# Two attention heads per output step, a ring of four score buffers, and other queues for the last stores

## What is computed

```python
z = jnp.einsum('bqhd,bkhd->bhqk', qblk, k) * scale + bias
mask = key_idx[None, :] < qpos[:, None]
log_1mb = jnp.where(mask, jax.nn.log_sigmoid(-z), 0.0)
acc = lax.cumsum(log_1mb, axis=3, reverse=True) - log_1mb
wts = jnp.where(mask, jnp.exp(jax.nn.log_sigmoid(z) + acc), 0.0)
return jnp.einsum('bhqk,bkhd->bqhd', wts, v)
```

## Time and profile before

| | us |
|---|---|
| median of 3 runs | 2250.02 |
| lowest and highest | 2247.71, 2251.95 |
| the profiled execution, its own time | 2249.7 |
| its span, first to last instruction | 2248.1 |
| mean granted TensorE clock | 0.986 of full |
| PE busy | 2185.9 (97%) |
| DVE busy | 1068.2 (48%) |
| ACT busy | 770.7 (34%) |
| POOL busy | 67.7 (3%) |
| `stick()` on PE, from `score(0)` to the end of `sample_outputs` | about 1698.6 to 1792.3 |

### The profile page before, as it was taken

One profiled execution on the slowest core, in us unless ns is written; L12 is line 12 of the kernel. 1 busy time (PEld: TensorE's weight loads), 2 busy tenths in 40 slices (PEclk: granted clock), 3 DMA queues, 4 the chain that ended last, 5 costly groups with the idle time before them and its releaser, 6 DMA issues.

```text
span 2248.1 us, 44698 instructions
## 1 busy us (share of the span) xinstructions
PE 2185.9 (97%) x18380; PEld 2124.4 (94%) x18380; DVE 1068.2 (48%) x1534; ACT 770.7 (34%) x1062; POOL 67.7 (3%) x143
## 2 busy tenths in 40 slices
PE   8999999999988999999999999999999899999996
PEld 7999999998877899999999999999996599999996
DVE  5444433586455554444334444433568444444332
ACT  5222222335244442222223222222357543222222
POOL 0000000100100000000000000000103200000000
PEclk9999999999988999999999999999999999999998
DMA  4333333432300332333233233323324323333331
GB/s 133 97 89 88 91 94 79 123 85 76 81 2 2 90 93 86 93 93 91 88 93 94 86 91 93 89 88 95 99 76 142 114 76 104 93 93 88 90 94 47
DMA packets 353651, 197.89 MB, mean 88 GB/s; under 512 B 10054, under 2 KB 348130, under 8 KB 353544
## 3 DMA queue, kind: packets, MB, share of 16 engines
q1 hardware_dynamic: 344640, 172.36, 26.6%
q0 software_dynamic: 6736, 21.97, 3.2%
q10 hardware_dynamic: 2176, 2.15, 0.3%
HBM read 188.52 MB, written 8.05 MB: 87 GB/s over the span
## 4 chain that ended last, share of the span: by engine, by line
PE 91%; DVE 4%; ACT 2%; issue 2%; DMA 1%; POOL 0%; DVEq 0%; ACTq 0%; POOLq 0%
PE PS L2174 81%; PE PS L2282 5%; PE PS L2849 1%; DVE wlo L1382 1%; PE PS L2768 0%; PE PS L2782 0%; DVE rawE L1419 0%; PE PS L2751 0%; PE PS L2834 0%; DVE tmp L1504 0%; PE PS L2654 0%; DMA tmp<-q_rows 0%; PE PS L2350 0%; PE PS L2189 0%; DMA prow_f<-in_ln_ffn 0%
## 5 line engine op out<-in xcount | busy, mean ns | idle before, releaser
L2174 PE MATMUL PS<-hh,whi 128*128 128x260 f32 x3600 | 730.9, 284 | 2.9 <-DVE hl L2099 1.7
L2174 PE MATMUL PS<-hh,wlo 128*128 128x260 f32 x3600 | 727.2, 284 | 0.0
L2174 PE MATMUL PS<-hl,whi 128*128 128x260 f32 x3600 | 726.3, 283 | 0.0
L1382 DVE TENSOR_TENSOR wlo<-stage,whi 128x1024 fp32r<-128x1024 f32 x337 | 412.3, 1223 | 449.5 <-ACT whi L778 439.7
L2174 PEld LDWEIGHTS PS<-hh,whi 128*128 128x128 f32 x3600 | 557.4, 189 | 5.8 <-DVE small L1521 1.5
L2174 PEld LDWEIGHTS PS<-hh,wlo 128*128 128x128 f32 x3600 | 556.6, 189 | 0.0
L2174 PEld LDWEIGHTS PS<-hl,whi 128*128 128x128 f32 x3600 | 555.2, 189 | 0.0
L778 ACT ACTIVATE whi<-stage 128x1024 fp32r<-128x1024 f32 x337 | 352.7, 1048 | 269.9 <-PE PS L2174 263.0
L2174 PE MATMUL PS<-act_h,whi 128*128 128x260 f32 x1408 | 284.3, 283 | 0.0
L2174 PE MATMUL PS<-act_h,wlo 128*128 128x260 f32 x1408 | 283.5, 283 | 0.0
L2174 PE MATMUL PS<-act_l,whi 128*128 128x260 f32 x1408 | 282.8, 282 | 0.0
(11 more groups left out here) (431 smaller groups left out, 1573.1 us busy)
## 6 DMA issues: line engine op xcount, KB each, us to landing
stage<-in_ffn_w_gate SPq DMA_DIRECT2D x88, 512.0 KB, 3.8
stage<-in_ffn_w_up SPq DMA_DIRECT2D x88, 512.0 KB, 3.8
stage<-in_ffn_w_down SPq DMA_DIRECT2D x64, 512.0 KB, 4.0
stage<-in_w_in_e SPq DMA_DIRECT2D x28, 512.0 KB, 3.8
stage<-in_ffn_w_down SPq DMA_DIRECT2D x32, 384.0 KB, 3.4
stage<-in_w_in_o SPq DMA_DIRECT2D x20, 512.0 KB, 3.7
stage<-in_w_out_e SPq DMA_DIRECT2D x8, 512.0 KB, 3.6
stage<-in_w_out_o SPq DMA_DIRECT2D x8, 512.0 KB, 3.6
```

The lines of the kernel that those rows point to most:

```text
L1382: dve.tensor_tensor(wlo[:, slot, :], stage[:, s % STAGE_SLOTS, :], whi[:, slot, :].bitcast(F32), ALU.subtract).then_inc(lo_ready, 1)
L2174: mm = pe.matmul(psum[:, half, :], w, x(k)[:, half * HALF:(half + 1) * HALF], start=first and w is hi and x is rhs_hi, stop=last and w is lo)
```

## The change

Three edits.

1. Outputs of heads 2m and 2m+1 are made together, `output(m)`, on PE after `sums(h)` of the next even head h = 2m+2 (the last pair within `sample_outputs`). For each of the four widths, the product of the even head (lower 64 partitions of bank 6) stands next to that of the odd head (upper 64). ACT then copies 128 partitions once per pair. As a head's weights now live longer, `skZ` becomes a ring of four, and `skL` moves to another place in memory to make room. `sample_outputs` is cut 4 and 4 around the last pair, where it was 2 and 6 around the last head.
2. POOL stores the prompt's values and keys in turn 6 of its loop, not in turn 4, that is behind the load of the last query row.
3. `y_prompt` is stored by SP in four quarters, not by POOL in two halves, and `y_sample` by SP after them. The copies to `ysrow` are made by DVE, not ACT.

```diff
-                    if n == TS // 2:
+                    if n == TS - 2:
                         pool.wait_ge(v_rows, 1 + NB)
                         save(o["sbv_p"][0, 0].rearrange("(c p) h d -> p c (h d)", p=P), vtok[:])
...
-                    if h >= 3:
-                        act.wait_ge(sk_o, h - 2)
-                    act.activation(skZ[:, h % 3, :], banks(0, 3)[:, 0:SCORES], ACT.Identity, bias=sbb[:, 0, h:h + 1])\
+                    if h >= 4:
+                        act.wait_ge(sk_o, h - 3)
+                    act.activation(skZ[:, h % 4, :], banks(0, 3)[:, 0:SCORES], ACT.Identity, bias=sbb[:, 0, h:h + 1])\
...
+                def output(m):
+
+                    act.wait_ge(sk_o, 2 * m + 2)
+                    act.activation(prO[:, OQ + m, 0:TP], banks(6, 1), ACT.Copy).then_inc(sk_oc, 1)
+                    act.wait_ge(sk_oc, m + 1)
+                    act.activation(oO[:, OK + m, 0:TP], prO[:, OQ + m, 0:TP], ACT.Copy).then_inc(o_hi, 1)
...
-                    if h >= 1:
-                        output(h - 1)
+                    if h >= 2 and h % 2 == 0:
+                        output(h // 2 - 1)
...
-                def output(h):
+                def output(m):
 
-                    r = slice(h % 2 * HDC, (h % 2 + 1) * HDC)
-                    if h:
-                        pe.wait_ge(sk_oc, h)
-                    pe.wait_ge(sk_w, h + 1)
+                    if m:
+                        pe.wait_ge(sk_oc, m)
+                    pe.wait_ge(sk_w, 2 * m + 2)
                     for c, (at, w) in enumerate(SCORE):
-                        mm = pe.matmul(banks(6, 1)[r, c * P:TP], vtok[:, c, h * HDC:(h + 1) * HDC],
-                                       skZ[:, h % 3, at:at + w], start=c == 0, stop=c == NB - 1)
-                    mm.then_inc(sk_o, 1)
+                        for q in range(2):
+                            h, r = 2 * m + q, slice(q * HDC, (q + 1) * HDC)
+                            mm = pe.matmul(banks(6, 1)[r, c * P:TP], vtok[:, c, h * HDC:(h + 1) * HDC],
+                                           skZ[:, h % 4, at:at + w], start=c == 0, stop=c == NB - 1)
+                            if c == NB - 1:
+                                mm.then_inc(sk_o, 1)
...
-                sample_outputs(0, 2)
-                output(HC - 1)
-                sample_outputs(2, TS)
+                sample_outputs(0, 4)
+                output(KC - 1)
+                sample_outputs(4, TS)
...
+            for a in range(4):
+                sp.wait_ge(y_row, KD // 4 * (a + 1))
+                part = slice(a * DM // 4, (a + 1) * DM // 4)
+                sp.dma_start(o["y_prompt"][0].rearrange("(b p) n -> p b n", p=P)[:, :, part], yrow[:, :, part])\
+                  .then_inc(stored, 16)
+            sp.wait_ge(ys_row, 2)
+            sp.dma_start(o["y_sample"][:, 0, :], ysrow[:]).then_inc(stored, 16)
+            sp.wait_ge(stored, 80)
```

More of the change, by code:

```diff
@@ L332, in build_step @@
         of_sample = sb("of_sample", [P, PAGES, TS], F32, st)
+        skL = sb("skL", [P, SCORES], F32, st)
         st.close()
@@ L336, in build_step @@
         VALUE_BANKS, KEY_BANKS = (3, 4, 5, 7), (6, 3, 4, 5)
-        skL = sb("skL", [P, SCORES], F32, st)
         skX = sb("skX", [P, 2, SCORES], F32, st)
-        skZ = sb("skZ", [P, 3, SCORES], F32, st)
+        skZ = sb("skZ", [P, 4, SCORES], F32, st)
         skR = sb("skR", [P, 3 * P], F32, st)
@@ L411, in build_step @@
             sem(n) for n in "gate_read gate_ready up_read prod_ready act_hi act_lo".split())
-        y_row, stored = sem("y_row"), sem("stored")
+        y_row, ys_row, stored = sem("y_row"), sem("ys_row"), sem("stored")
         y_t, SETUP_T = setup_t, 4 + KD
@@ L753, in _ @@
                     mix_o()
[L754 to L760, removed]
             if ("mix_e", 0) in STAGES:
@@ L1257, in softplus_parts @@
                         act.wait_ge(sk_sp, h)
-                    link(act.activation(skL[:], skZ[:, h % 3, :], ACT.Abs))
+                    link(act.activation(skL[:], skZ[:, h % 4, :], ACT.Abs))
                     link(act.activation(skL[:], skL[:], ACT.Exp, scale=-1.0))
@@ L1264, in weights @@
                     act.wait_ge(sk_sub, h + 1)
-                    act.activation(skZ[:, h % 3, :], skZ[:, h % 3, :], ACT.Exp).then_inc(sk_w, 1)
-                def output(h):
-                    r = slice(h % 2 * HDC, (h % 2 + 1) * HDC)
[L1270 to L1274, removed]
+                    act.activation(skZ[:, h % 4, :], skZ[:, h % 4, :], ACT.Exp).then_inc(sk_w, 1)
+                def output(m):
[3 more added lines that the diff above has]
+                    act.activation(oO[:, OK + m, 0:TP], prO[:, OQ + m, 0:TP], ACT.Copy).then_inc(o_hi, 1)
                 act.preload_act_table_set(LN_EXP)
@@ L1366, in _ @@
                    .then_inc(y_row, 1)
-            for a in range(2):
-                act.activation(ysrow[:, a * 512:(a + 1) * 512], banks(4 + a, 1)[0:TS, :], ACT.Copy).then_inc(y_row, 1)
         @block.vector
@@ L1999, in softplus @@
                         dve.wait_ge(sk_acc, h)
-                    link(dve.scalar_tensor_tensor(out=sp, in0=skZ[:, h % 3, :], scalar=0.0, in1=skL[:],
+                    link(dve.scalar_tensor_tensor(out=sp, in0=skZ[:, h % 4, :], scalar=0.0, in1=skL[:],
                                                   op0=ALU.max, op1=ALU.add))
@@ L2028, in stick @@
                     dve.wait_ge(sk_acc, h + 1)
-                    dve.tensor_tensor(skZ[:, h % 3, :], skZ[:, h % 3, :], banks(3, 3)[:, 0:SCORES], ALU.subtract)\
+                    dve.tensor_tensor(skZ[:, h % 4, :], skZ[:, h % 4, :], banks(3, 3)[:, 0:SCORES], ALU.subtract)\
                        .then_inc(sk_sub, 1)
@@ L2151, in _ @@
             last_norm()
+            dve.wait_ge(y_t, SETUP_T + KD)
+            for a in range(2):
+                dve.tensor_copy(ysrow[:, a * 512:(a + 1) * 512], banks(4 + a, 1)[0:TS, :]).then_inc(ys_row, 1)
         @block.tensor
@@ L2773, in sums @@
                     mm.then_inc(sk_acc, 1)
-                def output(h):
-                    r = slice(h % 2 * HDC, (h % 2 + 1) * HDC)
-                    if h:
-                        pe.wait_ge(sk_oc, h)
-                    pe.wait_ge(sk_w, h + 1)
-                    for c, (at, w) in enumerate(SCORE):
-                        mm = pe.matmul(banks(6, 1)[r, c * P:TP], vtok[:, c, h * HDC:(h + 1) * HDC],
-                                       skZ[:, h % 3, at:at + w], start=c == 0, stop=c == NB - 1)
-                    mm.then_inc(sk_o, 1)
+                def output(m):
+                    if m:
+                        pe.wait_ge(sk_oc, m)
+                    pe.wait_ge(sk_w, 2 * m + 2)
+                    for c, (at, w) in enumerate(SCORE):
+                        for q in range(2):
[4 more added lines that the diff above has]
+                                mm.then_inc(sk_o, 1)
                 score(0)
```

## The result

| us | before | changed |
|---|---|---|
| median (4 runs each) | 2250.78 | 2234.09 |
| lowest to highest | 2247.71 to 2251.95 | 2231.90 to 2235.52 |
| profiled execution, its span | 2248.1 | 2232.3 |

The ratio is 0.9927, 95% interval 0.9910 to 0.9944.

A forecast was written before the change was run, and what follows sets the result against it. PE holds 91% of the chain, bound together with DVE in heads 2 and 3. Loop 7.6 plus end 2.6 is 10.2 us off the profiled 2249.7: 2239.5, as median 2239.8, stated as 2240; range 2236 to 2244.5.

The forecast's parts named there:

- The pairs overlap: Head outputs on PE: products into lower and upper 64 partitions run together, 2.3 us a pair; no overlap, 4.6, had 3%.
- Heads 1 to 4 are bound by DVE: Loop, heads 1 to 4: DVE needs 9.19 us per head, nothing saved; PE waits about 2.2 us before sums(2) and sums(4).
- the clock's rival: Loop: clock falls in PE's new waits, 2.1 us each at sums(5) to sums(7), little at sums(2), sums(4); 2242 to 2245; 14%.
- Heads 4 to 7: Loop from head 4: query-row wait, low clock and one output go, ACT holds back 1.6; sums(6) 5.7 us earlier.
- The loop's end: Behind sums(7): 9.3 us of PE work (samples, last pair, samples) instead of 11.27, saving 1.9.
- The end: Program's end: last landing at 2240.6 instead of 2243.2, saving 2.6 us (bounds 0.5 and 4); the 4.9 behind it stay.
- The landings' own term: Program's end: stores by SP in quarters and DVE's copies make the last landing 2.6 us sooner.
- Behind the loop PE takes the gain on in full: After the loop: PE is the bound to the end at a steady rate, so the loop's 7.6 us is kept.

The follow-up runs named there:

- POOL last: Changed kernel, where POOL too waits until all stores of y have landed, though it issues none: 0.9962 of before, 2240.55 us.
- the pairs alone: Kernel before with edit 1 alone (outputs of two heads made together), edits 2 and 3 undone: 0.9975 of before, 2243.30 us.
- the halves apart: Changed kernel with the two loops of output(m) exchanged, the even head's four products first, then the odd one's: 0.9959 of before.
- PE kept busy: Changed kernel with products nobody reads in three waits of PE and the first half of the samples' rows copied earlier: 0.9924 of before, 2230.81 us.
- the second one: Second comparison: the changed kernel, unaltered, timed once more against the kernel before: 0.9947, 2236.61 us.

## Why the prediction was wrong, point by point

- *The pairs overlap*, 2.3 us each: right. Rows of the kernel before, in which another stage did the same, had shown it, and the exchanged loops confirm it.
- *Heads 1 to 4 are bound by DVE*, so the new waits of PE cost and bring nothing: right, 1.9 us each where 2.2 were forecast. At `sums(4)` the clock fell, as the clock's rival had it, and that sum took 5.3 us in place of 3.65. It cost little, as that rival also said, but it made PE the later of the two: `sums(5)` started without a wait, some 0.3 us after DVE's part was ready.
- *Heads 4 to 7*: `sums(5)` started 56.83 us after the loop's start, forecast 56.82. That is luck: the forecast let it wait for DVE, and it came behind PE's own work at the low clock. `sums(6)` came 6.2 us sooner after the loop's start, forecast 5.7; ACT's last logarithm ended 0.5 sooner than forecast and so held it back by less.
- *The loop's end*: from `sums(7)` to L2839 (L2843 before) 13.68 us now, 15.66 before; 2.0 saved, forecast 1.9.
- *The end*: here it failed, at the step "the span ends at 2248.1, 4.9 later, where nothing is recorded, and I leave these 4.9 as they are". They were not a constant of every program but POOL's drain, 4.40 us of them, and edit 3 took POOL off the end. The landings' own term was 2.6, and 3.2 were measured in this pair of profiles, 1.8 by the means of all. I had read the views of busy work and of DMA, in which sequencers' drains have no row; the source view of the barrier's line has one.
- *Behind the loop PE takes the gain on in full*: not quite. At `out_o0` the clock fell in both profiles of the changed kernel and gave back 1.5 and 3.1 us, and 1.5 with POOL last. With the pairs alone and with the halves apart that stretch was 53.85, as in before. The rival on the clock looked for it only inside the loop.
- *Not from the change*: the loop started 1.6 us sooner in the first profile. Over the ten profiles of this study that start lies between 1693.76 and 1698.66, with the same instructions before it. Most of the difference arises in the mixer of layer 0, between the norms at 415 and 817 us: 402.2 us in before, 401.0 in the changed kernel, 397.8 with PE kept busy. The clock falls there in different places. The same sixteen instructions, in before and then with PE kept busy:

```profile
646.88 3.30 PE L2282 MATMUL PS<-prE 128*128 128x128 f32 x16
```

```profile
644.57 1.95 PE L2276 MATMUL PS<-prE 128*128 128x128 f32 x16
```

From 600 to 720 us the mean clock is 0.86 in before, 0.87 in the changed kernel and 0.91 with PE kept busy. Why it falls in one execution and not in another stays open.

In the sum: 8.1 + 7.6 - 1.5 + 1.6 = 15.8 us of span, where 10.2 were forecast; 4.4 of the difference is the drain. Without it the time would lie within the range. That it lies below the range took, beside the drain, some luck in this comparison: an early start, a short low stretch and early landings, as its profile shows them. In the second one, where these were less kind, the kernel took 2236.61.

## What to carry to other kernels

When a span ends long after the last landing, ask which engine's program ends last and how long its drain is, before the stretch is written off as fixed; here it cost 4.4 us (5.4 with POOL last again) only because POOL was the one to wait for the stores. Letting SP issue and wait moved it under other work; letting SP only wait brought 2.5 us in the profile, as the drain then took 7.47. Matrix products of 64 output partitions are worth interleaving in the program's order, lower half next to upper half: the same sixteen instructions took 2.3 us so and 3.9 us one half after the other. Where PE must wait just ahead of a long dense stage, a few products that nobody reads can be cheaper than the low clock after it.

## What the runs showed of the hardware

- POOL's drain at the end of a program: 4.40 us after its own stores had landed (three profiles), 5.37 behind its small stores in the middle of PE's work (five profiles), the same 5.37 when it had issued none for 465 us, 7.47 when its stores were under way. SP's took 0.007, DVE's, ACT's and PE's 0.6 to 1.7.
- The granted clock was low at `out_o0` after a wait of only 0.79 us and products of 8 columns. At `sums(4)` of the changed kernel it fell within the first 1.2 us of work after a wait of 1.89; with the halves apart the wait was 1.89 as well and the clock stayed high. The length of one wait did not decide it.
- Stores of 512 KB by SP: from the issue of the last quarter, with the samples' rows behind it, to SP going on, 3.2 to 5.1 us passed in six profiles (2228.6 to 2232.0 in the changed kernel, 2232.9 to 2238.0 with the halves apart).
